# Feed-forward layers: token sums, order of the layer's end, and the first lora rows of a two-layer hybrid encoder step

## The reference, cut to what matters

```python
def rms_norm(x, g):
    y = x32 * lax.rsqrt(jnp.mean(x32 * x32, axis=-1, keepdims=True) + RMS_EPS)
    return (y * g.astype(jnp.float32)).astype(x.dtype)

def swiglu_ffn(x, w_gu, w_down):
    gate, up = jnp.split(x @ w_gu, 2, axis=-1)
    return (jax.nn.silu(gate) * up) @ w_down

for layer in range(DEPTH):
    ...                                   # mixer: x += mixer(rms_norm(x))
    hp = hp + swiglu_ffn(rms_norm(hp, norm_ffn[layer]), ffn_w_gu[layer], ffn_w_down[layer])
y = rms_norm(h, norm_final)
```

## Time and profile before

| | |
|---|---|
| time, median of 3 runs | 3634.82 us (3629.58 to 3637.86) |
| the profiled execution's own time | 3635.43 us |
| span of the profile | 3633.7 us |
| mean granted TensorE clock | 0.979 |
| PE busy | 3392.1 us, 93% |
| VectorE busy | 1740.1 us, 48% |
| GpSimd busy | 1676.2 us, 46% |
| ScalarE busy | 1348.6 us, 37% |
| DMA queue 1 | 216.58 MB, 21.3% of 16 engines' span |
| gate and up weight loads | 168 of 256 KB, 2.9 us each to landing |

### The profile page before, as it was taken

One profiled execution on the slowest core, in us unless ns is written; L12 is line 12 of the kernel. 1 busy time (PEld: TensorE's weight loads), 2 busy tenths in 40 slices (PEclk: granted clock), 3 DMA queues, 4 the chain that ended last, 5 costly groups with the idle time before them and its releaser, 6 DMA issues. The chain is left out here.

```text
span 3633.7 us, 86414 instructions
## 1 busy us (share of the span) xinstructions
PE 3392.1 (93%) x32938; PEld 2920.7 (80%) x32938; DVE 1740.1 (48%) x3399; ACT 1348.6 (37%) x2895; POOL 1676.2 (46%) x1510
## 2 busy tenths in 40 slices
PE   8999878888886989999999899999989899999998
PEld 7999767777775978888888787777769888888887
DVE  6212557766663374444444533333343744444444
ACT  5212444454442132333333434444443333333234
POOL 5443345554551534555545544344433345545454
PEclk9999989999997999999999999999999999999999
DMA  4422101111102211111111144444441111111111
GB/s 150 153 90 86 66 23 38 40 45 38 46 18 93 89 37 46 43 45 46 45 46 43 68 99 96 108 100 93 103 107 65 37 46 43 45 46 45 46 43 72
DMA packets 433026, 234.96 MB, mean 65 GB/s; under 512 B 191012, under 2 KB 417076, under 8 KB 431847
## 3 DMA queue, kind: packets, MB, share of 16 engines
q1 hardware_dynamic: 429170, 216.58, 21.3%
q10 hardware_dynamic: 3572, 14.33, 1.0%
HBM read 188.28 MB, written 47.80 MB: 65 GB/s over the span
## 5 line engine op out<-in xcount | busy, mean ns | idle before, releaser
L2498 DVE TENSOR_TENSOR H<-ps,H 128x512 f32<-128x512 f32 x608 | 419.7, 690 | 482.4 <-PE ps L2186 481.7
L2070 POOL TENSOR_TENSOR split<-work,split 128x512 fp32r<-128x512 f32 x280 | 381.5, 1368 | 507.3 <-ACT split L2343 500.2
L2186 PE MATMUL ps<-split,split 128*128 128x512 f32 x1824 | 516.7, 391 | 4.0 <-DVE split L2502 4.0
L2239 PE MATMUL ps<-xs,split 128*128 128x512 f32 x1920 | 511.8, 393 | 1.6 <-POOL split L2070 1.6
L1229 PE MATMUL ps<-arena 64*64 64x64 f32 (+2 forms) x8800 | 432.0, 237 | 51.2 <-DVE arena L1655 15.3
L2239 PEld LDWEIGHTS ps<-xs,split 128*128 128x128 f32 x1920 | 349.9, 188 | 70.7 <-POOL split L2070 2.0
L2186 PEld LDWEIGHTS ps<-split,split 128*128 128x128 f32 x1824 | 339.7, 188 | 78.8 <-issue 4.9
L1229 PEld LDWEIGHTS ps<-arena 64*64 64x64 f32 x8800 | 325.2, 137 | 87.0 <-issue 35.4
L2239 PE MATMUL ps<-split,split 128*128 128x512 f32 x1440 | 374.0, 395 | 0.4 <-ACT ps L2381 0.4
L3083 PE MATMUL ps<-xs,split 128*128 128x384 f32 x1656 | 359.8, 354 | 2.6 <-POOL split L2997 2.6
L602 PE MATMUL ps<-mixed,wsplit_mix 128*128 128x384 f32 x1872 | 334.1, 340 | 10.7 <-DVE mixed L814 10.3
(11 more groups left out here) (316 smaller groups left out, 5891.0 us busy)
## 6 DMA issues: line engine op xcount, KB each, us to landing
work<-in_ffn_w_gu SPq DMA_DIRECT2D x168, 256.0 KB, 2.9
work<-in_ffn_w_down SPq DMA_DIRECT2D x168, 128.0 KB, 2.4
work<-in_cache_v SPq DMA_DIRECT2D x64, 256.0 KB, 3.9
work<-in_cache_k SPq DMA_DIRECT2D x256, 64.0 KB, 2.2
rkv_scratch<-lora ACTq DMA_DIRECT2D x24, 576.0 KB, 2.8
stage_mix<-in_rwkv_w_rkv SPq DMA_DIRECT2D x24, 512.0 KB, 3.7
work<-in_attn_w_qkv SPq DMA_DIRECT2D x24, 512.0 KB, 4.1
h_scratch<-H SPq DMA_DIRECT2D x2, 4608.0 KB, 12.5
```

The source lines that it names most:

```text
L2070: pool.tensor_tensor(w[1], frm, w[0].bitcast(F32), ALU.subtract).then_inc(u_lo, 1)
L2186: last = pe.matmul(full(DOWN + j % 2), w[part][:, (m % 2) * P:(m % 2 + 1) * P], mem.hid[xpart][:, SEG[h]], start=(a == 0), stop=(a == 2))
L2239: last = pe.matmul(full(to), unit(i)[part][:, k * P:(k + 1) * P], operand[xpart][:, k, :], start=(first and k == 0 and a == 0), stop=(k == ...
L2498: dve.tensor_tensor(at, full(DOWN + j % 2), at, ALU.add).then_inc(added, 1)
```

## The change

What it does, by place:
- Start of a feed-forward phase. VectorE makes B11's sum before the norm's writes instead of after the hidden parts; GpSimd makes B21's sum behind its first two low parts, while the norm runs. T3's combination moves behind the hidden parts, T3's low parts behind the last of the 24 additions. The additions start right behind the six differences; T4's differences stand one at a time among them. Products 3 and 4 wait for 2 and 6 low parts instead of 4. ScalarE casts T3 after the first down block, T1 before the fourth down block.
- Last turn and tail. Unit 7 is split before the down weights. The transpose is done behind quarter k = 0 (looped turns) or k = 1 (last turn) of product 7 instead of before it. The last down block is loaded into A12 after unit 7, not into A21 after unit 6. `leave(0)` and `leave(1)` are called inside the last turn, around `m1`.
- Layer 0's tail. The casts of the attention's first two weight tiles go from GpSimd to ScalarE (`next_high`), one in the last turn, one after the square of k = 4; GpSimd's subtractions come ahead of its norm additions. Their loads are issued in another order.
- Front. The high and low part of k = 0 are made for the first seven row groups (SOON columns) before the last two groups are done.
- Memory: the token operands start 8 elements lower and the norm's buffers at their start.

```diff
@@ -661,10 +663,13 @@
...
                     leave_h(i - 1)
+            act.wait_ge(xn_out, ROWS - 2)
+            act.wait_ge(pads_ready, 2)
+            act.copy(padded[0][:, 0, 0:SOON], mem.xnp[:, 0, 0:SOON]).then_inc(wa_hi_soon, 1)
             act.wait_ge(xn_out, ROWS)
-            act.wait_ge(pads_ready, 2)
             for k in range(KB):
-                act.copy(padded[0][:, k, :], mem.xnp[:, k, :]).then_inc(wa_hi_x, 1)
+                cols = slice(0 if k else SOON, TPAD)
+                act.copy(padded[0][:, k, cols], mem.xnp[:, k, cols]).then_inc(wa_hi_x, 1)
                 if k == 1:
...
@@ -790,13 +795,17 @@
...
                     dve.tensor_copy(pads[:, :, :, 0], mem.vec[:, :, NV:NROW]).then_inc(pads_ready, 1)
+            dve.wait_ge(xn_out, ROWS - 2)
+            dve.wait_ge(pads_ready, 2)
+            dve.wait_ge(wa_hi_soon, 1)
+            dve.tensor_tensor(padded[1][:, 0, 0:SOON], mem.xnp[:, 0, 0:SOON], padded[0][:, 0, 0:SOON].bitcast(F32), ALU.subtract).then_inc(wa_lo_soon, 1)
             leave_x(ROWS - 1)
...
             dve.wait_ge(xn_out, ROWS)
-            dve.wait_ge(pads_ready, 2)
             for k in range(KB):
+                cols = slice(0 if k else SOON, TPAD)
                 dve.wait_ge(wa_hi_x, k + 1)
-                dve.tensor_tensor(padded[1][:, k, :], mem.xnp[:, k, :], padded[0][:, k, :].bitcast(F32), ALU.subtract).then_inc(wa_lo, 1)
+                dve.tensor_tensor(padded[1][:, k, cols], mem.xnp[:, k, cols], padded[0][:, k, cols].bitcast(F32), ALU.subtract).then_inc(wa_lo, 1)
             dve.tensor_copy(mem.shiftcol[:, :, 0], mem.xnp[:, :, TP]).then_inc(col_ready, 1)
...
@@ -2041,16 +2052,20 @@
...
             sp.dma_start(mem.raw[:, A11, :], down[(HB - 1) * P:HB * P, 0:512]).then_inc(raw_in[A11], 16)
+            def load_next(j):
+                wqkv = t["attn_w_qkv"][0].rearrange("(k p) m -> p k m", p=P)
+                sp.dma_start(mem.raw[:, 2 * j:2 * j + 2, :].rearrange("p s (k m) -> p (s k) m", k=4), wqkv[:, :, j * D:j * D + P]).then_inc(next_in[j], 16)
+
             sp.wait_ge(u_lo, split_no(6, TURNS))
-            sp.dma_start(mem.raw[:, A21, :], down[(HB - 1) * P:HB * P, 512:1024]).then_inc(raw_in[A21], 16)
+            if layer == 0:
+                load_next(1)
+            sp.wait_ge(u_lo, split_no(7, TURNS))
+            sp.dma_start(mem.raw[:, A12, :], down[(HB - 1) * P:HB * P, 512:1024]).then_inc(raw_in[A12], 16)
             sp.wait_ge(d_lo, 4 * TURNS + 3)
...
             if layer == 0:
-                wqkv = t["attn_w_qkv"][0].rearrange("(k p) m -> p k m", p=P)
-                for j, u in ((1, 1), (0, 0)):
-                    sp.wait_ge(u_lo, split_no(7, TURNS))
-                    sp.wait_ge(d_lo, 4 * TURNS + (5 if j else 4))
-                    sp.dma_start(mem.raw[:, 2 * j:2 * j + 2, :].rearrange("p s (k m) -> p (s k) m", k=4), wqkv[:, :, u * D:u * D + P]).then_inc(next_in[j], 16)
+                sp.wait_ge(d_lo, 4 * TURNS + 5)
+                load_next(0)
             else:
...
@@ -2098,6 +2113,8 @@
...
             low_plain(1)
+            for r in range(2):
+                pool.tensor_tensor(part(T4F, r), part(B21[0], r).bitcast(F32), part(B21[1], r).bitcast(F32), ALU.add).then_inc(xp_ready, 1)
             pool.wait_ge(norm.lo_done, KB)
...
@@ -2127,25 +2144,19 @@
...
             s2_s4(TURNS)
-            for i in (3, 5, 6):
+            for i in (3, 5, 6, 7):
                 low(i, TURNS)
...
             low_last(0)
-            low(7, TURNS)
             low_last(1)
...
             if layer == 0:
-                chain = Chain(pool, next_hi)
                 for n, j in enumerate((1, 0)):
-                    after.pool(pool, n)
                     w = mem.wsplit_next[:, j]
                     frm = mem.raw[:, 2 * j:2 * j + 2, :].rearrange("p s n -> p (s n)")
-                    pool.wait_ge(next_in[j], 16)
-                    pool.wait_ge(p_done, product_no(6, TURNS))
-                    pool.wait_ge(m1_ready, HB)
-                    pool.wait_ge(d_lo, 4 * TURNS + 6)
-                    chain.link(pool.tensor_scalar(w[:, 0, :], frm, 1.0, None, ALU.mult))
+                    pool.wait_ge(next_hi, n + 1)
                     pool.tensor_tensor(w[:, 1, :], frm, w[:, 0, :].bitcast(F32), ALU.subtract).then_inc(next_split, 1)
+                    after.pool(pool, n)
             else:
...
@@ -2240,6 +2251,9 @@
...
                             last.then_inc(p_done, 1)
+                        if k == turn_at:
+                            pe.wait_ge(r_product, g)
+                            pe.transpose(RTURN, hf[:, SEG[2]], mem.ident[:, :]).then_inc(r_done, 1)
                         fill(fills[k])
...
@@ -2265,10 +2279,11 @@
...
                 product(SA, 2, B21, False, (1, 0, 1, 1))
-                pe.wait_ge(t_lo, 4)
+                pe.wait_ge(t_lo, 2)
                 product(SB, 3, T2, False, (0, 1, 0, 3))
...
                     y_turn(0)
+                pe.wait_ge(t_lo, 6)
                 pe.wait_ge(copied_c, g)
...
@@ -2278,9 +2293,7 @@
...
                 product(SA, 5, T4, False, (0, 1, 0, 1))
-                pe.wait_ge(r_product, g)
-                pe.transpose(RTURN, hf[:, SEG[2]], mem.ident[:, :]).then_inc(r_done, 1)
-                product(SC, 7, B22, False, (0, 1, 0, 2))
+                product(SC, 7, B22, False, (0, 1, 0, 2), 0 if downs else 1)
                 if not downs:
...
@@ -2385,6 +2398,17 @@
...
                 act.copy(mem.ysb, full(Y + n)).then_inc(y_copied, 1)
+
+            def next_high(j):
+                act.wait_ge(next_in[j], 16)
+                act.copy(mem.wsplit_next[:, j][:, 0, :], mem.raw[:, 2 * j:2 * j + 2, :].rearrange("p s n -> p (s n)")).then_inc(next_hi, 1)
+
+            def next_first(k):
+                if k == 4:
+                    act.wait_ge(p_done, product_no(6, TURNS))
+                    act.wait_ge(m1_ready, HB)
+                    act.wait_ge(d_lo, 4 * TURNS + 6)
+                    next_high(0)
...
@@ -2403,10 +2427,10 @@
...
                 copy_bank(SA, SB, 4, silu0_ready, copied_a, g)
+                high(7, g, (p_done, product_no(4, g)))
                 if last:
...
                     high_last(0)
-                high(7, g, (p_done, product_no(4, g)))
                 act.wait_ge(r_done, 3 * g - 1)
...
@@ -2423,6 +2447,9 @@
...
                     last_high(2, r_turned, g)
+                    if layer == 0:
+                        act.wait_ge(p_done, product_no(5, g))
+                        next_high(1)
                 else:
...
@@ -2452,12 +2479,12 @@
...
             high_plain(3)
-            t_high(T3F, T3, 1)
             hid_high(0, m0_ready, 1, None)
...
             high_down(0, 1, None)
+            t_high(T3F, T3, 1)
             high_down(1, 2, None)
...
@@ -2466,20 +2493,23 @@
...
             high_down(2, 3, (down_done, 6))
-            high_down(3, 4, (down_done, 12))
             act.wait_ge(plain_done, 15)
             t_high(T1F, T1, 3)
+            high_down(3, 4, (down_done, 12))
             high(4, 1, (plain_done, 15))
             high_down(0, 5, (down_done, 18))
-            act.wait_ge(t_lo, 6)
+            act.wait_ge(t_lo, 4)
             t_high(T4F, T4, 7)
-            hid_high(0, m0_ready, 2, (down_done, 24))
+            hid_high(0, m0_ready, 2, (down_done, 23))
             high_down(1, 6, (down_done, 24))
...
             turn(TURNS, True)
-            after.scalar(act)
+            if layer == 0:
+                after.scalar(act, next_first)
+            else:
+                after.scalar(act)
...
@@ -2546,6 +2576,12 @@
...
                 dve.tensor_tensor(h, full(DOWN + n).rearrange("p (k n) -> p k n", k=4), h, ALU.add).then_inc(y_added, 1)
+
+            def leave(n):
+                c, k = divmod(n, KB)
+                h = mem.H[:, k, c * CW:(c + 1) * CW]
+                dve.wait_ge(tail_done, n + 1)
+                dve.tensor_tensor(h, tail_bank(n), h, ALU.add).then_inc(h_done, 1)
...
@@ -2569,13 +2605,14 @@
...
                 c12(g)
-                if not last:
+                if last:
+                    leave(0)
+                else:
                     hid_low(2, hid_no(2, g + 1))
...
                 if last:
+                    leave(1)
                     last_low(1, 3)
-
-            part = lambda ap, r: ap[:, 2 * r:2 * r + 2, :]
...
@@ -2594,66 +2631,57 @@
...
             norm.inverse(dve, 2)
+            value(B11, T2F)
             norm.split(dve, 2)
...
             value(B22, T3F)
+            plain_product_2(0, 6)
             value(B12, T1F)
-            for r in range(2):
-                dve.wait_ge(xf_ready, 3 + r)
-                combine(T3F, T1F, T3F, r)
-            plain_product_2(0, 6)
             hid_low(0, 1)
...
             hid_low(1, 3)
-            value(B11, T2F)
             for r in range(2):
                 dve.wait_ge(xf_ready, 5 + r)
+                combine(T3F, T1F, T3F, r)
+            for r in range(2):
```

(54 more changed lines are left out.)

20 lines of the change are left out of this document (12 added, 8 removed).

## The result

The changed kernel takes **3599.57 us** (median of 4 runs, 3590.21 to 3600.37) against 3636.20 for the kernel before in the same comparison (4 runs), a ratio of 0.9893 with an interval of 0.9873 to 0.9913: 36.6 us less. The profiled execution took 3598.85 us (span 3597.1, mean granted clock 0.981), so the two profiled spans differ by 36.6 us too.

The account below looks back on a forecast made before the run. Mid-layer TensorE was busy 597.98 of 600 us, so only waits and half clock at the layers' two ends, plus the front, were winnable. 8.4 + 7.3 + 6.5 + 2.2 + 1.3 = 25.7 us off 3635.4 gave 3609.5, range 3601 to 3621.

Parts of the forecast that it names:

- part 2: Looped turns: moving the transpose behind product 7's first quarter costs 0; room before product 6 shrinks from 4.0 to 3.3 us.
- Part 1: Start of both layers' feed-forward: shorter waits and less half clock gain 8.4 us in layer 0, 7.3 in layer 1.
- (a): Layer start: B11's and B21's sums collide on VectorE and GpSimd, norm's writes begin 1.3 us late, charged in full.
- (b): Plain blocks: VectorE's first addition comes at 1320.0 instead of 1327.82; TensorE waits about 0.6 us for it.
- (c): Plain blocks, later additions: only GpSimd's turns show among VectorE's operations, 0.7 us in all (bounds 0 and 3).
- (d): Entry to the turns: T3's low parts behind the last addition; nothing booked, bounds 1 us gained and 2 lost per layer.
- Part 3: End of both layers: shorter waits, and in layer 0 less half clock, gain 6.5 us in layer 0, 2.2 in layer 1.
- Part 4: Front: early high and low parts for seven of nine row groups shorten TensorE's 4.11 us wait; gain 1.3 us.
- R1: Plain blocks: VectorE stays the bound, half of both waits stay, 8.5 us, giving 3618; chance 0.19.
- R2: Half clock stays although the waits shrink, taking back 5.6 us, giving 3615; chance 0.12.
- R3: Plain blocks: the first addition did not release TensorE, Part 1 gives nothing, 10.0 us are left, 3625.4; chance 0.07.
- R4: Looped turns: product 6 waits for the moved transpose's copy, costing 60 us over 38 turns, 3669.5; chance 0.04.

Follow-up runs that it names:

- s_start: Kernel before with only the new order at the start of both feed-forward phases; ratio to before 0.9972, 10.2 us less.
- v_peel: Changed kernel with VectorE's first turn written out, T4's low parts behind that turn's second and fourth additions; 3590.84 us, ratio to before 0.9861.
- t_turn: Kernel before with only the transpose moved into product 7, in looped and last turns; ratio to before 1.0005.
- e_end: Kernel before with only the changes at the layers' ends, the transpose staying ahead of product 7; ratio to before 0.9980, 7.3 us less.
- x_align: Kernel before with only the token operands (and norm's buffers) 32 bytes lower; ratio to before 0.9965, 12.7 us less.
- v_b21: Changed kernel with B21's two sums back on VectorE, none on GpSimd; its starts are 85.2 us in both layers, 2.6 and 2.1 longer.

## Why the prediction was right in its sign and short in its size

**The step that failed is a line of the diff that has no term in the sum: XT_AT.** The front text names it ("the token operands start 8 elements lower"), part 2 costs the looped turns at 0 for the transpose alone. It was worth 11 us by the trace, 12.7 by the clock (8 to 17.5). I had read 38 turns x 132 matmuls as "busy at full clock: nothing can be won", yet the earlier trace rows only say that TensorE never waited. 597.98 us busy of 600 is not 597.98 us at pace; the means of 395 against 393 ns in two groups of the same shape stood on the page before, and I did not ask why. With the address priced, 25.7 + 11.0 = 36.7 us; measured 36.6. That the rest fits so well is partly luck, as its terms show.

**Part 1, start: 15.7 predicted, 11.3 in the trace, 12.6 in s_start's, 10.2 by its time.** Layer 1's 4.8 would be 1.6 more but for half clock in its first 48 matmuls, which no step of the change explains (10.16 us where layer 0's take 8.56, and the kernel before's 8.59 in layer 1). (a) The collision of the sums cost 1.06 us (1.3 predicted); TensorE felt all of it, as argued.

(b) and (c) were too timid: the waits of 0.6 and 0.7 us came as 0.23, since six back-to-back differences lost no turn to GpSimd. The rule that an operation of GpSimd costs VectorE its whole length failed there. The window shrank by 11.1 and 10.1 us; less the 1.06, that is 10.1 and 9.0 against 8.4 and 7.3.

(d) took more than that back, and was booked at 0. I set the first addition's end at 10.5 us after the plain blocks against a third tile reached at 11.0. Both ends were wrong. The 11.0 was the old arrival in the kernel before (2909.31 - 2898.34 in layer 1), with two waits in it, of 0.47 us and of 2.02 us:

```profile
2898.81 0.73 PE L2301 MATMUL ps<-xs 128*128 128x512 f32 x2 [0.47 <-DVE work L2512]
...
2909.31 0.84 PE L2186 MATMUL ps<-split,split 128*128 128x512 f32 x3
```

The second of them I had just counted as gone, and the first went too, so the new arrival is 8.2 (1349.75 - 3.81 - 1337.70). And the addition ended at 12.0. The four low parts are not the reason: with GpSimd's turns they took 3.45 + 3.40 = 6.9 us, where my count allowed 4 x 1.15 + 3 x 1.2 = 8.2. But they began only 2.9 us after the plain blocks (1340.60), behind the last of the 24 additions and two hidden low parts, and the memsets (1.0) and one more hidden low part (0.6) stand among them and the first addition. The difference is the 3.81 us. With half clock behind it (a clock of 0.60 from 1350 to 1356 us) the entry cost 10.1 - 6.5 = 3.6 us in layer 0 and 9.0 - 4.8 - 1.6 = 2.6 in layer 1, beyond my bound of 2. v_peel shows it by taking it away.

**Part 2, order: right.** t_turn is 1.0005, and the room before product 6 sufficed.

**Part 3, end: 8.7 predicted, 10.4 in the trace** (7.5 and 2.9), 7.3 from e_end, which lacks the transpose. The weights' wait went; the sums' wait shrank by 1.16 (1.2 predicted); the wait behind the tail by 2.60 (2.6 predicted): VectorE's two subtractions no longer met GpSimd. The 1.7 us of half clock came back in the changed kernel, but not in e_end, where 12 matmuls at 2061.7 us took 3.77 us instead of 2.33: that term was a chance and not a saving.

**Part 4, front: 1.3 predicted, 1.45 in the trace.** By the rule that the prediction weighed (the Trainium skill, "SBUF — State Buffer", "SBUF: two separate sides") it would have been 0.8. The trace does not agree with the rule here: VectorE's early piece began at 35.47 us and took 1.08, though GpSimd's TENSOR_SCALAR ran from 33.29 to 36.06. Nothing shows the other 3.4 us of the stretch before the first feed-forward to be the change's: the same code took 1275.1, 1280.0, 1281.0 and 1279.3 us up to there in four kernels with the front of before (before, s_start, e_end, x_align), depending on where half clock fell: from 400 to 450 us the mean clock is 0.97 in the kernel before and 0.83 in the other three, and there they fall 4 to 5 us behind it. Over all kernels here the stretch took 1272 to 1281 us with the old front and 1270 to 1278 with the new one.

**The rivals.** R1 (VectorE the bound) is refuted by the windows, and v_b21 shows how near it is: two operations more, and the waits are 1.86 and 1.72 us. R2 (half clock stays) was right in kind and wrong in place: clock 1.00 in the plain blocks, 0.60 behind the new wait. R3 and R4 did not happen. The front text calls semaphores the only thing that holds one engine for another; the 5.81 and 3.57 us above are VectorE and GpSimd holding each other without one. None of the rivals, and no bound, covered a change in TensorE's pace, so the range ended at 3601 on the fast side.

## What to carry to other kernels

A busy engine is not an engine at pace: where two groups of one shape differ in their mean, find out why before you call a stretch untouchable, and give every line of a diff a term, the addresses too. When a wait is removed, every later arrival moves by it: compare a new release time with the new arrival, not with the one in the old trace. Work that is moved out of one queue's crowded stretch to the edge of a loop lands in the next crowded one; writing out the first turn for one engine costs only instructions and lets it be spread there.

## What the runs showed of the hardware that I had not expected

- The pace of a stream of 512-column matmuls depends on how far the streamed operand lies from the weight tiles: 226.7 ns from start to start at multiples of 256 bytes (50176, 50432), most of them 228 to 237 ns at 128, 192, 224 and 32 bytes beyond; the whole program is 12.7 us (8 to 17.5) faster for it. The distance counts, not the address, and 384-column matmuls show no difference (354 and 355 ns). After a switch from 256 to 512 columns five matmuls are slow even at good distances.
- VectorE and GpSimd do not always take turns. Six 128x1024 operations of VectorE, one right behind the other, kept GpSimd's 0.73 us operation waiting until they were through (3.57 us, in both layers), whereas operations that start about together take turns (5.81 and 5.70 us for two each).
- The stretch up to the first feed-forward varied from 1270 to 1281 us between profiled runs of nearly the same code. A term of half clock of 1 or 2 us in one trace is no saving that can be booked.
